# Odd mixer: the last channel tile's conv taps moved from GpSimd to VectorE, attention heads stored in partition halves, conv norm sums placed after the second attention slot

## What is computed

```python
def odd_mixer(x, w_in, forget_b, dw_w, dw_b, cn_g, cn_b, w_out):
    p = x @ w_in                                  # 1024 -> 3*512 + 8 + 2*512
    q, k, v = ...                                 # 8 heads of 64, from the first 1536 columns
    log_f = jax.nn.log_sigmoid(p[..., 3 * D_C:3 * D_C + H_C] + forget_b)
    y_c = forgetting_attention(q, k, v, log_f).reshape(bsz, s, D_C)
    y_d = conformer_conv(p[..., 3 * D_C + H_C:], dw_w, dw_b, cn_g, cn_b)
    return jnp.concatenate([y_c, y_d], axis=-1) @ w_out

def conformer_conv(p_d, dw_w, dw_b, cn_g, cn_b):
    h = p_d[..., :D_D] * jax.nn.sigmoid(p_d[..., D_D:])
    h = causal_dwconv(h, dw_w) + dw_b             # 31 taps, 512 channels
    h = layer_norm(h, cn_g, cn_b)                 # over the 512 channels
    return jax.nn.silu(h)
```

## Time and profile before

| | us |
|---|---|
| three runs | 1386.91, 1388.94 (median), 1389.70 |
| the profiled execution, whole | 1390.78 |
| its span in the profile | 1388.9 |
| PE busy in the span | 1269.3 (91%) |
| DVE busy | 804.8 (58%) |
| ACT busy | 577.3 (42%) |
| POOL busy | 259.9 (19%) |

### The profile page before, as it was taken

How to read it: one execution, slowest core, us unless ns; L and a number is a source line. 1 busy time by engine, 2 the same in 40 slices (tenths; PEclk the granted TensorE clock), 3 DMA queues, 4 the chain that set the end, 5 groups by cost and what they waited for, 6 DMA issues and landing times.

```text
span 1388.9 us, 23065 instructions
## 1 busy us (share of the span) xinstructions
PE 1269.3 (91%) x9496; PEld 1178.6 (85%) x9496; DVE 804.8 (58%) x1182; ACT 577.3 (42%) x874; POOL 259.9 (19%) x198
## 2 busy tenths in 40 slices
PE   5799999999976789899998998999989968999997
PEld 2699877779954579899998988999989957999996
DVE  2767844436446577654436676555456996555544
ACT  3332433334532313444235445444345555544433
POOL 1233300045430011000200040111001972111100
PEclk9799999999988899999999999999999989999999
DMA  9556211115530004455133534555543304355551
GB/s 390 219 211 265 98 61 61 61 61 182 182 121 1 0 31 168 158 183 184 48 122 124 185 146 145 185 182 183 184 152 122 122 31 152 124 183 182 183 190 47
DMA packets 27473, 195.56 MB, mean 141 GB/s; under 512 B 3192, under 2 KB 3328, under 8 KB 3968
## 3 DMA queue, kind: packets, MB, share of 16 engines
q1 hardware_dynamic: 26496, 191.90, 38.6%
q10 hardware_dynamic: 896, 2.50, 0.5%
HBM read 193.33 MB, written 1.05 MB: 140 GB/s over the span
## 4 chain that ended last, share of the span: by engine, by line
PE 79%; DVE 13%; ACT 4%; issue 1%; POOL 0%; ACTq 0%; DVEq 0%
PE ps L401 23%; PE ps L403 23%; PE ps L402 23%; PE ps L443 3%; PE ps L608 3%; DVE acc L1908 3%; DVE w_lo L1406 1%; PE ps L540 1%; DVE V L1647 1%; PE ps L458 1%; DVE xconv L1512 1%; DVE rstd L1717 1%; ACT w_hi L859 1%; DVE wexp L1650 1%; PE ps L596 1%
## 5 line engine op out<-in xcount | busy, mean ns | idle before, releaser
L1406 DVE TENSOR_TENSOR w_lo<-ring,w_hi 128x1024 fp32r<-128x1024 f32 x288 | 359.1, 1257 | 330.5 <-ACT w_hi L859 325.3
L859 ACT ACTIVATE w_hi<-ring 128x1024 fp32r<-128x1024 f32 x312 | 327.0, 1058 | 491.2 <-PE ps L403 412.0
L401 PE MATMUL ps<-x_hi,w_hi 128*128 128x256 f32 x1216 | 349.8, 288 | 20.2 <-DVE x_lo L1726 20.2
L402 PE MATMUL ps<-x_lo,w_hi 128*128 128x256 f32 x1216 | 348.6, 287 | 0.0
L403 PE MATMUL ps<-x_hi,w_lo 128*128 128x256 f32 x1216 | 348.4, 286 | 0.0
L401 PEld LDWEIGHTS ps<-x_hi,w_hi 128*128 128x128 f32 x1216 | 238.0, 196 | 22.5 <-issue 22.5
L402 PEld LDWEIGHTS ps<-x_lo,w_hi 128*128 128x128 f32 x1216 | 237.9, 196 | 0.0
L403 PEld LDWEIGHTS ps<-x_hi,w_lo 128*128 128x128 f32 x1216 | 237.7, 196 | 0.0
L401 PE MATMUL ps<-g_hi,w_hi 128*128 128x256 f32 x608 | 171.0, 281 | 2.5 <-POOL g_lo L1350 1.1
L403 PE MATMUL ps<-g_hi,w_lo 128*128 128x256 f32 x608 | 170.2, 280 | 0.0
L402 PE MATMUL ps<-g_lo,w_hi 128*128 128x256 f32 x608 | 169.4, 279 | 0.0
(11 more groups left out here) (299 smaller groups left out, 2157.7 us busy)
## 6 DMA issues: line engine op xcount, KB each, us to landing
ring<-in_weights SPq DMA_DIRECT2D x156, 1024.0 KB, 4.9
o_sb<-in_weights SPq DMA_DIRECT2D x10, 1024.0 KB, 6.5
z_sb<-in_weights SPq DMA_DIRECT2D x10, 1024.0 KB, 7.0
V<-in_weights SPq DMA_DIRECT2D x3, 1024.0 KB, 22.6
dft<-in_dft ACTq DMA_DIRECT2D x1, 1026.0 KB, 5.1
X<-in_x SPq DMA_DIRECT2D x1, 1024.0 KB, 4.9
ctx_room<-in_ctx SPq DMA_DIRECT2D x1, 1024.0 KB, 7.7
xconv<-in_weights SPq DMA_DIRECT2D x1, 1024.0 KB, 27.2
```

Source lines behind the costliest of these rows:

```text
L401: mm(dst, w_h, x_h, start=start, stop=False, skip_group_check=True)
L402: mm(dst, w_h, x_l, start=False, stop=False, skip_group_check=True)
L859: do(w_hi[:, q % 2, part], ring[:, q % RING, part], ACT.Copy).then_inc(S("hi_ready"), 1)
L1406: v.tensor_tensor(w_lo[:, q % 2, part], ring[:, q % RING, part], w_hi[:, q % 2, part], ALU.subtract).then_inc(S("lo_ready"), 1)
```

## The change

The fourth conv tile leaves POOL. DVE does all 31 taps of all four tiles; `convolved` now lags tile 2 by two and tile 3 by four taps, so each k issues four taps, one per tile. `lo` of `odout`+2 and +3 moves to DVE as well. POOL does nothing in the mixer.

`attend(hd)` takes only its own head's 64 value columns and writes them to its own 64 partitions of the same 256 columns, so that rounding and splitting an attention tile take one instruction of 128 partitions each.

PE sums the conv's mean after `mixed_slot(1)`, directly ahead of the variance; before, it stood in the middle of `mixed_slot(0)` and the variance ahead of `mixed_slot(1)`. ACT's and DVE's orders are rewritten to go with it.

```diff
@@ TensorE: attend(hd)
-                at = SEQ * b
-                mm(ps[:, c % 2, at:at + SEQ], vtok[:, 0, c * P:(c + 1) * P], probT[:, b, 0, :],
+                part, own = slice(FD * b, FD * (b + 1)), slice(FD * hd, FD * (hd + 1))
+                mm(ps[part, c % 2, 0:SEQ], vtok[:, 0, own], probT[:, b, 0, :],
                    start=True, stop=False, skip_group_check=True)
-                mm(ps[:, c % 2, at + P:at + SEQ], vtok[:, 1, c * P:(c + 1) * P], probT[:, b, 1, P:SEQ],
+                mm(ps[part, c % 2, P:SEQ], vtok[:, 1, own], probT[:, b, 1, P:SEQ],
                    start=False, stop=True, skip_group_check=True).then_inc(S("attn_done"), 1)
@@ TensorE: mixed_slot(0) and what follows it
-                        pe.wait_ge(S("probT_moved"), 7)
-                        column_sum(conv_mean, ones_h[:, :], lambda k: acc31[:, k, :], KH, S("norm_in"),
-                                   S("norm_mean"), since("in", "conv"))
...
             mixed_slot(0)
             for hd in range(6, FH):
                 attend(hd)
+            mixed_slot(1)
+            column_sum(conv_mean, ones_h[:, :], lambda k: acc31[:, k, :], KH, S("norm_in"),
+                       S("norm_mean"), since("in", "conv"))
             column_sum(conv_var, ones_h[:, :], lambda k: sq[:, k, :], KH, S("norm_squares"),
                        S("norm_var"), since("squares", "conv"))
-            mixed_slot(1)
             mixed_slot(2)
             mixed_slot(3)
@@ ScalarE
             def round_attention(c):
                 act.wait_ge(S("attn_done"), 2 * c + 2)
-                chain.step(do(g_hi[0:FD, KH + c, :], ps[0:FD, c % 2, 0:SEQ], ACT.Copy))
-                do(g_hi[FD:P, KH + c, :], ps[FD:P, c % 2, SEQ:2 * SEQ], ACT.Copy).then_inc(S("attn_rounded"), 1)
+                do(g_hi[:, KH + c, :], ps[:, c % 2, 0:SEQ], ACT.Copy).then_inc(S("attn_rounded"), 1)
...
+            weighed(3)
             hi(STARTS["odout"])
             move_odin(8)
-            exponentials(4)
-            weighed(3)
-            exponentials(5)
             for hd in range(2):
                 move_turned(hd)
-            exponentials(6)
+            for hd in range(4, 7):
+                exponentials(hd)
@@ GpSimd: the whole chain of taps, and
-            for q in range(STARTS["odout"] + 2, STARTS["odout"] + 4):
-                pool.wait_ge(S("lo_ready"), 2 * q)
-                lo(q)
@@ VectorE
             def convolved(k0, k1):
                 for k in range(k0, k1):
                     taps(k, (0, 1))
                     if k >= 3:
                         taps(k - 2, (2,))
+                    if k >= 5:
+                        taps(k - 4, (3,))
...
-                for b in range(2):
-                    part = slice(FD * b, FD * (b + 1))
-                    ins = v.tensor_tensor(g_lo[part, KH + c, :], ps[part, c % 2, SEQ * b:SEQ * (b + 1)],
-                                          g_hi[part, KH + c, :], ALU.subtract)
...
+                v.tensor_tensor(g_lo[:, KH + c, :], ps[:, c % 2, 0:SEQ], g_hi[:, KH + c, :], ALU.subtract)\
+                    .then_inc(S("attn_split"), 1)
...
+            lo(STARTS["odout"] + 1)
+            convolved(21, 25)
+            for c in range(2, KH):
+                split_attention(c)
+            convolved(25, TAPS - 1)
```

More of the change, by code:

```diff
@@ L1269, in _ @@
             round_attention(2)
+            round_attention(3)
+            hi(STARTS["odout"] + 2)
             for k in range(KH):
@@ L1279, in _ @@
                 do(sq[:, k, :], acc31[:, k, :], ACT.Silu, bias=vcol("cn_b", k)).then_inc(S("conv_whole"), 1)
-            hi(STARTS["odout"] + 3)
             hi(STARTS["odout"] + 4)
@@ L1965, in _ @@
             gated_unit(3)
+            first_tap(3)
             dve.wait_ge(S("forget_done"), 1)
@@ L1990, in _ @@
                 sum_inverse(hd)
-            convolved(16, 18)
+            convolved(12, 14)
             maximum(3)
-            convolved(18, 19)
-            lo(STARTS["odout"])
-            convolved(19, 20)
+            convolved(14, 15)
             maximum(4)
@@ L1999, in _ @@
             maximum(6)
-            convolved(20, 21)
+            lo(STARTS["odout"])
             sum_inverse(4)
             sum_inverse(5)
-            convolved(21, 22)
+            convolved(15, 16)
             sum_inverse(6)
-            convolved(22, 24)
+            convolved(16, 18)
             split_attention(0)
-            convolved(24, 25)
+            convolved(18, 19)
             maximum(7)
-            convolved(25, 26)
+            convolved(19, 20)
             sum_inverse(7)
-            convolved(26, 28)
+            convolved(20, 21)
             split_attention(1)
-            convolved(28, TAPS - 1)
-            dve.wait_ge(S("pool_order"), 2 * POOL_TAPS - 1)
-            late = range(POOL_TAPS, TAPS - 1)
-            for k in late:
-                if k > late[2]:
-                    chain.join()
-                taps(k, (3,))
-                if k in late[:2]:
-                    taps(TAPS - 3 + k - POOL_TAPS, (2,))
-                if k - POOL_TAPS in (2, 3, 4):
-                    final_tap(k - POOL_TAPS - 2)
+            lo(STARTS["odout"] + 1)
[3 more added lines that the diff above has]
+            convolved(25, TAPS - 1)
+            taps(TAPS - 3, (2,))
+            taps(TAPS - 5, (3,))
+            final_tap(0)
+            taps(TAPS - 2, (2,))
+            taps(TAPS - 4, (3,))
+            final_tap(1)
+            chain.join()
+            taps(TAPS - 3, (3,))
+            final_tap(2)
+            chain.join()
+            taps(TAPS - 2, (3,))
             chain.join()
             final_tap(3)
-            lo(STARTS["odout"] + 1)
+            lo(STARTS["odout"] + 2)
             dve.wait_ge(S("norm_mean"), since("mean", "conv") + 1)
@@ L2030, in _ @@
                     .then_inc(S("norm_centred"), 1)
-            for c in range(2, KH):
-                split_attention(c)
+            lo(STARTS["odout"] + 3)
             dve.wait_ge(S("norm_root"), since("root", "conv") + 1)
```

30 lines of the change are left out of this document (5 added, 25 removed).

## The result

The changed kernel takes 1392.5 us, the median of 11 runs (1391.8 to 1394.3), beside 1388.9 for the kernel before (11 runs, 1386.9 to 1390.8). The ratio is 1.0028, with an interval of 1.0019 to 1.0038: it is 3.6 us slower. The forecast was 1393.4 in a range of 1390.2 to 1396.8, with 0.78 on slower. Total and sign came out.

What follows compares the result with a forecast made beforehand. DVE's line up to the subtraction of the mean was taken as the bound: 3.3 us later there, then 4.4 later at 1171.9 in place of 1167.49; forecast 1393.4 us, 8 in 10 within 1390.2 to 1396.8.

Steps and rivals of the forecast that it cites:

- DVE's work, 66.9: DVE's line up to the subtraction of the mean: 66.9 us of work after, the same as 66.7 before.
- Waits, 1.9 + 2.8: DVE's waits on ACT: 1.93 ahead of `odin`+9 stays, new ones around `odout` and heads 4 and 5 add 2.8.
- Rival 1: DVE's new waits on ACT at `odout`, `odout`+1, heads 4 and 5 don't appear: -2.8, 1390.5 us; chance 0.12.
- Subtraction of the mean, +3.3: On DVE, the subtraction of the conv's mean starts at 1149.4, 3.3 us later than 1146.15.
- PE through both attention slots at 1142.5: PE finishes both attention slots at about 1142.5 and then waits for the last taps.
- Variance at half clock, 3.4: PE's column sum of the variance takes 3.4 us at half clock, 1.9 if not.
- Idle ahead of the conv slots, 5.35: Root, reciprocal, scale, SiLU and split between variance and first conv slot take 5.35 us as before, with PE idle.
- Four halves and the clock, 11.2 + 1.7: PE's four halves of conv slots take 2.80 each, 11.2 us, plus 1.7 lost to a low clock behind idle time.
- Contention, 11 us: Sharing with POOL costs DVE's line ahead of the subtraction about 11 us, which go when POOL is empty.
- Rival 2 and 3: DVE's taps: cheaper in a rotation of four, 1386.5 us, chance 0.05; or 0.44 even without POOL, 1397.9 us, chance 0.10.
- a subtraction before 1147: Sign of a wrong forecast: DVE's subtraction of the mean starting before 1147, as under rivals that shorten its line.
- the sign for "right": Signs of a right forecast include the subtraction at 1149 to 1150 and 2 to 4 us wait ahead of the first `attend`.

Runs made afterwards that it cites:

- act_old: The changed kernel with the orders of before around heads 3 to 6 on ScalarE and VectorE; 1394.0 us, ratio to before 1.0033.
- lo3_late: The changed kernel with the weight slot `odout`+3 behind the conv norm, not ahead of the root and reciprocal; 1391.3 us, ratio to before 1.0012.
- drop8: The changed kernel without 8 of the fourth tile's 31 taps; 1389.5 us, ratio to before 1.0003.
- dummy_pool: The changed kernel, with POOL doing the 24 taps of before again into spare rows nobody reads; 1402.2 us, ratio to before 1.0092.
- both_parts: The kernel before with only the fourth tile's taps on DVE and the heads in halves of the partitions; 1386.9 us, ratio to before 0.9984.

## Why the prediction came out, step by step

Times are taken from the stage's first row, 1071.75 before and 1070.26 after.

- **DVE's work, 66.9.** From 1076.40 to 1146.73 are 70.33, less the waits of 2.08, 0.37, 0.75, 0.64 and 0.52 is 65.97. Right to 0.9. Taps at 0.397 and slots at 2.28 held to the second digit. The forget gates were mis-sized: the 2.0 of the earlier trace rows held the contention, they took 1.37. I had cleared the taps of POOL's influence and forgot these.
- **Waits, 1.9 + 2.8.** 2.08, and 0.37 + 0.75 + 0.64 + 0.52 = 2.28. All of the kind and at the places named; ahead of `odout`+1 it was 0.52 and not 0.8, and the inverse sums of two heads waited, not one. Rival 1 (no new waits) is out.
- **Subtraction of the mean, +3.3.** It stands at 76.47 after and at 74.40 before: +2.07. From 3.3 to there: -0.93 for the work, -0.52 and +0.15 for the waits, +0.06 for the line's start (0.46 later, 0.4 said).
- **PE through both attention slots at 1142.5.** It was at 1139.75 (the 1.95 ahead of 1141.70), 1141.2 on the scale of before. The wait ahead of the first `attend` was said as 2 to 4 and is 1.39; the stall of 3.13 ahead of 1132.36, for an attention split behind 16 taps on DVE, wasn't named at all. Neither shows in the stage of this kernel, since PE waits for the mean anyway. `act_old` shows where this ends: a stall of 3.29 at the same `attend` reaches DVE through the logits.
- **Square to PE, 0.92.** 0.91.
- **Variance at half clock, 3.4.** Wrong: 2.00, at a clock of 1.00. This is the first step that failed. I took it that PE's standing still on both sides of the mean has the clock down at the variance. It was down for the mean's own sum (0.50 from 1143 to 1146) and back at 1.00 when the variance began.
- **Idle ahead of the conv slots, 5.35.** Wrong: 6.54. The second failure. The prediction has the path from the variance as before, and no term for `lo(odout+3)`, which the change puts on DVE between the subtraction and the reciprocal. `lo3_late` took 1.65 of the 6.54 away. The 4.89 left there is what the norm's path takes undisturbed; the 5.35 held rows of before in which the reciprocal stood behind an attention split and the scale beside POOL.
- **Four halves and the clock, 11.2 + 1.7.** 1169.16 - 1156.18 = 12.98. Right. Stretches of 2 us behind the 6.54, PE after:

```profile
1156.00:1158.00 2.00, 1.82 (x8) 0.50 0.19 78
1158.00:1160.00 2.00, 2.00 (x12) 0.52 0.00 0
1160.00:1162.00 2.00, 2.00 (x19) 1.00 0.00 0
```

From the subtraction to the residual's sum the prediction had 22.5 and the trace has 22.43, from -1.4 at the variance and +1.2 at the norm. What was forecast as +4.4 is +3.16 in the stage, all of the difference from DVE's line. The two failures hang together: DVE's slot holds the time from variance to conv slot at 8.54, with a variance of 2.00, 2.51 or 3.12 (`drop8`, `act_old`), and the prediction had 3.4 + 5.35 = 8.75 by another way. That the two are near is luck, and a reader shouldn't take that part as confirmed.

- **Contention, 11 us.** `dummy_pool` has 11.28 of DVE's busy time and 10.06 of the stage. Right.
- **Rival 2 and 3.** A tap is 0.397 and 0.396: neither cheaper in a rotation of four nor 0.44 without POOL. Both out.
- **The observation named for "wrong", a subtraction before 1147.** It stands at 1146.73 and would have said wrong; measured within the stage it is at 1148.2 of before's scale. An absolute time was a bad thing to name, where two executions differ by 1.5. On that scale it isn't between 1149 and 1150 either, as the sign for "right" wanted, and the wait of 2 to 4 ahead of the first `attend` is 1.39: these two signs missed.

What stays open: 1.23 of the 4.99 between `both_parts` and the change, and whether the halves still gain anything beside the moved taps: the stage of `both_parts` is 0.54 shorter than that of the taps alone, its median (1386.9) isn't.

## What to carry to other kernels

Where one engine's line of work ends last, put its independent pieces into the places where that engine waits, before moving work onto or off it; here the version that does so is 5.7 us faster than before, of which about 1.6 are such taps by the rows, and the rest is the taps' move, the halves, the two `attend`s and ACT's order. Moving 24 taps alone gave 1.3 to 2.4. A sum that another engine's chain waits for belongs ahead of the last big piece of work that can cover that chain, even if the wait ahead of the sum grows (12.43 for 1.95, and a stage 1.92 us shorter). And of each small work that is moved, look at what is queued behind it on its engine, and take costs for a quiet engine from rows that the neighbour didn't disturb.
